# Hybrid state-space, attention and expert layer in fp32: the order of loads and small operations in the opening, and the rotation angles ahead of the q and k norms

## The reference, cut to what matters

```python
xn = rms_norm(h, norm1_g)                    # rows of x scaled by 1/sqrt(mean square), times g
z = xn @ w_in                                # 1024 x 4096
u, q, k, v, g_ssm, g_att = split(z)          # 512 each for u, q, k, v, 1024 each for the gates
dt = exp(log_dt)                             # 32 groups of 64 states
abar = exp(a_re * dt) * (cos(a_im * dt) + i sin(a_im * dt))
bbar = (abar - 1) / a * b                    # complex
state[l] = abar * state[l-1] + bbar u[l]     # per group, along the tokens
y_ssm = Re(c state) + d * u, gelu, gated
q, k = rms_norm(q), rms_norm(k)              # per head and half, 64 wide
y_att = (softmax(q1 k1) - lam * softmax(q2 k2)) v
h = h + (sig(g_ssm) * (y_ssm @ w_proj_ssm) + sig(g_att) * (y_att @ w_proj_att)) @ w_out
y = h + experts(rms_norm(h))                 # 32 experts, 4 per token, swiglu
```

## Time and profile before

| what | value |
|---|---|
| median of three runs | 1146.06 us (1145.76 to 1146.14) |
| span of the profiled execution, first to last instruction | 1142.5 us |
| that execution's own time | not listed apart from the three runs; the median is 3.6 us above its span |
| PE busy | 1095.7 us (96%) |
| DVE, ACT, POOL busy | 298.4, 166.3, 34.1 us |
| DMA | 435.13 MB, mean 381 GB/s |
| chain that ended last | PE 58%, DMA 38%, DVE 2%, ACT 1% |

### The profile page before, as it was taken

How to read it: one execution, slowest core, us unless ns; L and a number is a source line. 1 busy time by engine, 2 the same in 40 slices (tenths; PEclk the granted TensorE clock), 3 DMA queues, 4 the chain that set the end, 5 groups by cost and what they waited for, 6 DMA issues and landing times.

```text
span 1142.5 us, 14277 instructions
## 1 busy us (share of the span) xinstructions
PE 1095.7 (96%) x5292; PEld 446.9 (39%) x5292; DVE 298.4 (26%) x804; ACT 166.3 (15%) x343; POOL 34.1 (3%) x51
## 2 busy tenths in 40 slices
PE   7999999999999999999999999999999999999997
PEld 4468887633333333333333333333333333333332
DVE  5987244242111111111111111111111111111111
ACT  3043440221111111111111111111111111111110
POOL 6020010000000000000000000000000000000000
PEclk9999999999999999999999999999999999999999
DMA  8734489999999999999999999999999999999996
GB/s 229 200 123 87 140 284 352 366 361 403 427 428 427 429 430 427 429 430 428 428 430 429 427 430 427 428 430 427 428 430 428 427 430 429 427 430 429 427 428 269
DMA packets 63578, 435.13 MB, mean 381 GB/s; under 512 B 19856, under 2 KB 28096, under 8 KB 38592
## 3 DMA queue, kind: packets, MB, share of 16 engines
q1 hardware_dynamic: 57776, 433.17, 92.6%
q0 software_dynamic: 608, 1.34, 0.6%
q10 hardware_dynamic: 5168, 0.27, 0.3%
HBM read 432.01 MB, written 1.57 MB: 380 GB/s over the span
## 4 chain that ended last, share of the span: by engine, by line
PE 58%; DMA 38%; DVE 2%; ACT 1%; issue 1%; SPq 0%; DVEq 0%; ACTq 0%
DMA arena<-in_w_up 38%; PE bank L1066 23%; PE bank L1111 9%; PE bank L635 5%; PE bank L673 4%; PE bank L619 3%; PE bank L1010 2%; PE bank L995 2%; PE bank L949 2%; PE bank L873 1%; PE bank L858 1%; PE bank L846 1%; DMA arena<-in_w_in 1%; PE bank L805 1%; PE bank L937 1%
## 5 line engine op out<-in xcount | busy, mean ns | idle before, releaser
L1066 PE MATMUL bank<-arena 128*64 128x512 f32 x2048 | 452.6, 594 | 30.2 <-DMA arena<-in_w_up 29.9
L1066 PEld LDWEIGHTS bank<-arena 128*64 128x64 f32 x2048 | 143.7, 137 | 331.8 <-issue 271.5
L1111 PE MATMUL bank<-arena 128*64 128x512 f32 x1024 | 226.8, 595 | 0.0
L1809 DVE TENSOR_SCALAR arena<-bank 128x256 f32<-128x256 f32 x64 | 27.2, 425 | 499.1 <-PE bank L1066 499.1
L1111 PEld LDWEIGHTS bank<-arena 128*64 128x64 f32 x1024 | 70.7, 137 | 133.9 <-issue 133.1
L1367 ACT ACTIVATE arena<-arena 128x256 f32<-128x256 f32 x64 | 26.6, 417 | 451.7 <-DVE arena L1810 451.7
L619 PEld LDWEIGHTS bank<-arena 128*128 128x128 f32 (+1 forms) x450 | 49.2, 143 | 89.6 <-issue 82.1
L619 PE MATMUL bank<-arena 128*128 128x128 f32 (+1 forms) x450 | 75.2, 290 | 8.9 <-DMA arena<-in_x 5.1
L1010 PE MATMUL bank<-arena 64*128 64x512 f32 x256 | 63.9, 616 | 0.7 <-ACT arena L1375 0.7
L995 PE MATMUL bank<-arena 128*64 128x512 f32 x248 | 60.1, 605 | 0.0
L1774 DVE TENSOR_SCALAR arena<-arena 128x128 f32 (+3 forms) x126 | 33.3, 327 | 92.7 <-issue 92.6
(11 more groups left out here) (294 smaller groups left out, 517.0 us busy)
## 6 DMA issues: line engine op xcount, KB each, us to landing
arena<-in_w_up SPq DMA_DIRECT2D x125, 2048.0 KB, 25.5
arena<-in_w_down SPq DMA_DIRECT2D x63, 2048.0 KB, 26.8
arena<-in_w_in SPq DMA_DIRECT2D x16, 1024.0 KB, 6.0
arena<-in_w_up SPq DMA_DIRECT2D x5, 1024.0 KB, 6.4
arena<-in_w_out SPq DMA_DIRECT2D x4, 1024.0 KB, 7.8
arena<-in_w_proj_ssm SPq DMA_DIRECT2D x8, 256.0 KB, 5.8
arena<-in_w_proj_att SPq DMA_DIRECT2D x2, 1024.0 KB, 7.9
arena<-in_w_down SPq DMA_DIRECT2D x2, 1024.0 KB, 31.6
```

What stands on the lines that cost most here:

```text
L1066: last = pe.matmul(B[n][64 * h:64 * h + 64, :], xg[:, 2 * j + r, :], rows[r][2 * h + n], start=False, stop=(j == order[-1] and r == 1), sk ...
L1111: last = pe.matmul(B[3][64 * n:64 * n + 64, :], (actT_last if last_block else actT)[:, k % 4, k // 4, :], dn_w[parity][k // 4][:, k % 4, 5 ...
L1809: TS(part(glu_t, n), v[:, 0], LIMIT, None, ALU.min)
```

## The change

ACT's queue: g is loaded as 8 rows of 128 (`g1_rows`, 512 bytes each); a_re, a_im and log_dt follow on the same queue and leave SP's. The first activation is Exp, and the Exp of dt stands ahead of the squares. The b loads are issued together after both roots. x_scale is copied after the wait for `trig` and the two Exps.

SP: token tile 0, first half of piece 0 (row blocks 0, 1; semaphore first_in), second half (2, 3), token tile 1, piece 1, then the c tables.

PE: turns g first, turns tile 0, runs piece 0 on tile 0 (block by block as the halves arrive), turns the small tables, then tile 1, and then runs piece 0 on it.

DVE: copies g out of the bank; a*dt stands between the products of tile 0 and tile 1; the lambda sums stand ahead of CR and CI; e8 and the angles n = 1 to 8 stand between WI and the norms of q and k, and n = 15 stays behind them.

```diff
@@ sync @@
-            for t in range(TT):
+            def load_x(t):
                 sp.dma_start(hx[:, t, :], a["x"][0, P * t:P * t + P, :]).then_inc(x_in[t], 16)
+            load_x(0)
+            for dst, src in first_pairs():
+                sp.dma_start(dst, src).then_inc(s["first_in"], 16)
             for dst, src in piece(0):
                 sp.dma_start(dst, src).then_inc(slot_in[0], 16)
-            for src, o in ((a["ssm_a_re"], 0), (a["ssm_a_im"], 1)):
-                sp.dma_start(natA[0:GG, o, :], src[0].rearrange("(g t) p -> g (t p)", t=2))\
-                  .then_inc(s["a_in"], 16)
-            sp.dma_start(dts[0:GG], a["ssm_log_dt"][0].rearrange("(g t) -> g t", t=2))\
-              .then_inc(s["a_in"], 16)
+            load_x(1)
+            for dst, src in piece(1):
+                sp.dma_start(dst, src).then_inc(slot_in[1], 16)
@@ tensor @@
+            pe.wait_ge(s["g1_in"], 16)
+            pe.transpose(B[7][:, 0:KT], g1_rows[0:KT, :], ident[0:KT, 0:KT]).then_inc(s["g1_ps"], 1)
...
-            z_piece(0, xT, 0, 0)
+            pe.wait_ge(s["xT"], 1)
+            pe.wait_ge(s["first_in"], 16)
+            for k in range(4):
+                if k == 2:
+                    piece_arrived(0)
+                pe.matmul(B[0][:, :], xT[:, k, 0:P], halves(0)[:, k, :], start=(k == 0), stop=False)
             pe.wait_ge(s["aT_in"], 1)
             transposes([(B[4][:, GG * i:GG * i + GG], natA[0:GG, i, :]) for i in range(4)])\
                 .then_inc(s["aT_ps"], 1)
-            pe.wait_ge(s["xT"], 4)
+            turn_x(1)
+            pe.wait_ge(s["xT"], 3)
             z_piece(0, xT, 1, 1)
@@ scalar @@
-            act.dma_start(g1, a["norm1_g"][0].rearrange("(k p) -> p k", p=P),
-                          allow_slow_non_contiguous=True).then_inc(s["g1_in"], 16)
+            act.dma_start(g1_rows[0:KT, :], a["norm1_g"][0].rearrange("(k p) -> k p", p=P)).then_inc(s["g1_in"], 16)
+            for src, o in ((a["ssm_a_re"], 0), (a["ssm_a_im"], 1)):
+                act.dma_start(natA[0:GG, o, :], src[0].rearrange("(g t) p -> g (t p)", t=2))\
+                    .then_inc(s["a_in"], 16)
+            act.dma_start(dts[0:GG], a["ssm_log_dt"][0].rearrange("(g t) -> g t", t=2))\
+                .then_inc(s["a_in"], 16)
             act.wait_ge(s["warm"], 1)
-            act.activation(warm, warm, ACT.Sqrt)
+            act.activation(warm, warm, ACT.Exp)
+            act.wait_ge(s["a_in"], 48)
+            act.activation(dts[0:GG], dts[0:GG], ACT.Exp).then_inc(s["dt"], 1)
...
             act.wait_ge(s["trig"], 1)
             act.activation(mg[:, 0, :], pa[:, 2, :], ACT.Exp)
             act.activation(mg[:, 1, :], pa[:, 2, :], ACT.Exp, scale=float(L))
+            act.wait_ge(s["scale_ps"], 1)
+            act.activation(x_scale, B[7][:, 0:TOK], ACT.Copy).then_inc(s["x_rs"], 1)
@@ vector @@
+            dve.wait_ge(s["g1_ps"], 1)
+            link(dve.tensor_copy(g1, B[7][:, 0:KT]))
+            for half in range(2):
+                turned(0, half)
             dve.wait_ge(s["dt"], 1)
...
             last.then_inc(s["aT_in"], 1)
+            x_variance(0)
+            for half in range(2):
+                turned(1, half)
+            x_variance(1)
...
             TTo(WIv, tAw, tBw, ALU.add).then_inc(s["win_t"], 1)
 
+            dve.wait_ge(s["xn"], 4)
+            link(dve.tensor_copy(e8r, cs))
+            link(dve.tensor_copy(e8i, sn))
+            for _ in range(3):
+                cmul(t16[0], t16[1], e8r, e8i, e8r, e8i, (GG,), scratch_2)
+                dve.tensor_copy(e8r, t16[0])
+                link(dve.tensor_copy(e8i, t16[1]))
...
+            for n in (1, 2, 4, 8):
+                angles(n)
 
             dve.wait_ge(s["q_sq"], 4)
...
+            angles(15)
```

More of the change, by code:

```diff
@@ L61 @@
  sig act aT2_ps aT2 ysb summed up_used dn_used bup_used dsel fin fin_out wr_in loop_z u_turn
- ahead_in up_tail dn_tail wg gated first_rows row_left row_right cT g1_in gate_ps out_ps rank routed o_read row_used up_half warm""".split()
+ ahead_in up_tail dn_tail wg gated first_rows row_left row_right cT g1_in gate_ps out_ps rank routed o_read row_used up_half warm g1_ps first_in""".split()
 def mixer_and_experts(nc, a, out):
@@ L208, in mixer_and_experts @@
         natA = at(158, 4, P)
+        g1_rows = at(199, P)
         lamrow = at(198, 4, SUB)
@@ L278, in piece @@
             slot = slot_of(i)
+            if i == 0:
+                w = a["w_in"][0].rearrange("(k p) n -> p k n", p=P)
+                return [(halves(0)[:, 2:4], w[:, 2:4, 0:512])]
             if i < 8:
@@ L301, in piece, with first_pairs @@
             return [(halves(i), w[:, 4 * (c % 2):4 * (c % 2) + 4, 512 * (c // 2):512 * (c // 2) + 512])]
+        def first_pairs():
+            w = a["w_in"][0].rearrange("(k p) n -> p k n", p=P)
+            return [(halves(0)[:, 0:2], w[:, 0:2, 0:512])]
         def pv(i):
@@ L359, in _ @@
                 arrived = last_in if i == PIECES - 1 else slot_in[i % RING]
-                if i > 0:
+                if i > 1:
                     for dst, src in piece(i):
                         sp.dma_start(dst, src).then_inc(arrived, 16)
-                else:
+                elif i == 0:
                     for n, half in enumerate((a["ssm_c_re"], a["ssm_c_im"])):
@@ L622, in _, with turn_x @@
             pe.wait_ge(s["ident"], 1)
-            for t in range(TT):
+            pe.wait_ge(s["g1_in"], 16)
+            pe.transpose(B[7][:, 0:KT], g1_rows[0:KT, :], ident[0:KT, 0:KT]).then_inc(s["g1_ps"], 1)
+            def turn_x(t):
                 pe.wait_ge(x_in[t], 16)
@@ L628, in _ @@
                         .then_inc(s["xT_ps"], 1)
-            pe.wait_ge(s["xT"], 2)
+            turn_x(0)
             def z_piece(i, tokens, bank, t):
@@ L653, in _ @@
                             for i in range(4)]).then_inc(s["cT_ps"], 1)
+            pe.wait_ge(s["xT"], 4)
             for t in range(TT):
@@ L1151, in _ @@
                 act.activation(xr[:, t:t + 1], xs[:, t:t + 1], ACT.Sqrt).then_inc(s["x_rs"], 1)
[L1152 to L1159, removed]
+            for dst, src in ((br_raw, a["ssm_b_re"]), (bi_raw, a["ssm_b_im"])):
+                act.dma_start(dst, src[0].rearrange("(g t) p h -> (t p) g h", t=2)).then_inc(s["b_in"], 16)
             act.wait_ge(s["trig"], 1)
@@ L1407, in turned, with x_variance @@
                     .then_inc(s["xT"], 1)
[L1409 to L1412, removed]
+            def x_variance(t):
                 x_rms = xs[:, t:t + 1]
@@ L1428, in _ @@
             last.then_inc(s["aT_in"], 1)
+            x_variance(0)
+            for half in range(2):
+                turned(1, half)
+            x_variance(1)
+            dve.wait_ge(s["x_rs"], 2)
+            for t in range(TT):
+                last = TS(diag[:, t, :], ident, xr[:, t:t + 1], None, ALU.mult)
+            last.then_inc(s["diag"], 1)
             dve.wait_ge(s["aT_ps"], 1)
@@ L1501, in _ @@
             cmul(bbr, bbi, br_raw, bi_raw, per_pair(cfr, H), per_pair(cfi, H), (GG, H))
+            dve.wait_ge(s["lam_in"], 64)
+            for i in range(2):
+                last = dve.tensor_tensor_reduce(lamrow[:, 2 * i, :], lamrow[:, 2 * i, :],
+                                                lamrow[:, 2 * i + 1, :], 1.0, 0.0, ALU.mult, ALU.add,
+                                                lamv[:, 2 + i:3 + i])
+            last.then_inc(s["lam_e"], 1)
             dve.wait_ge(s["cp_zero"], 1)
@@ L1532, in _, with angles @@
             TTo(WIv, tAw, tBw, ALU.add).then_inc(s["win_t"], 1)
[L1534 to L1539, removed]
+            dve.wait_ge(s["xn"], 4)
[5 more added lines that the diff above has]
+                link(dve.tensor_copy(e8i, t16[1]))
+            dve.memset(Rr[:, :, 0], 1.0)
+            dve.memset(Ri[:, :, 0], 0.0)
+            dve.tensor_copy(Rr[:, :, 1], e8r)
+            link(dve.tensor_copy(Ri[:, :, 1], e8i))
+            def angles(n):
+                cmul(Rr[:, :, n + 1:2 * n + 1], Ri[:, :, n + 1:2 * n + 1], Rr[:, :, 1:n + 1], Ri[:, :, 1:n + 1],
+                     per_pair(Rr[:, :, n], n), per_pair(Ri[:, :, n], n), (GG, n), scratch_2)
+            for n in (1, 2, 4, 8):
+                angles(n)
             dve.wait_ge(s["q_sq"], 4)
```

1 line of the change is left out of this document (removed).

## The result

The changed kernel takes 1158.39 us, the median of 4 runs (1157.75 to 1160.32), against 1145.91 (1145.29 to 1146.14) for the kernel before in the same comparison: ratio 1.0106, 95% interval 1.0093 to 1.0119. It is 12.5 us slower; the forecast was 1158.4. The profiled execution took 1157.75 us with a span of 1156.0.

The account below looks back on a forecast made before the run. DVE's norms, by 0.7 us over PE, were taken to bind at PE's turning of WR and WI. PE starting 10.4 later plus 1.9 for the clock gave +12.3: 1142.5 + 12.3 + 3.6 = 1158.4 us, range 1151.0 to 1160.5.

Parts of the forecast that it names:

- PE's lead at the end of gate tile 1: Opening: PE starts piece 0 sooner and gains 0.5 to 1.5 us, taken as 1.0, kept until it leaves gate tile 1.
- DVE's first product: Opening: DVE's first product, at 20.41 us in the kernel before, comes at about 19.2.
- block with POOL holding DVE: After win_t at 64.8: e8, squarings and angles, 8.1 us before, held by POOL's memset and copies, end at 79.2.
- norms behind it: After the angles: DVE's q and k norm work takes 5.7 us and ends at 84.9.
- PE starts turning: Turning of WR and WI: PE starts at 85.0 instead of 74.56, 10.4 us later.
- clock, over 40 blocks: Turning after about 12 us idle: PE resumes at 1.2 GHz and loses 1.9 us, bounds 1.0 and 2.6.
- shift of the span: Whole kernel: later PE start of 10.4 plus clock loss of 1.9 makes +12.3 us.
- The rival that the angles are hidden: PE's wait at 73.85: norms done before PE leaves gate tile 1, opening's gain kept, 1144.4 us; chance of faster 0.06.
- The rival without it: Moved block: DVE not held by POOL, PE starts at 78.7, +4.1 and +1.9 for the clock, 1152.1 us; chance 0.15.
- The rival that turning keeps the clock low: Turning: transposes do not raise the clock, all 40 blocks run slow, 4.4 us instead of 1.9, 1160.9 us; chance 0.03.
- DVE's long chain gains 1.2: Opening: DVE's long chain of products starts 1.2 us earlier, bounds 0 and 2.0.
- Uniform shift: From PE's start at 74.56 on: everything, expert loads included, moves by the same amount; w_up waits keep their length.

Follow-up runs that it names:

- experiment 1: Changed kernel with e8 and angles n = 1 to 8 moved back behind the q and k norms: 1144.01 us, ratio 0.9984 to the kernel before.
- experiment 2: Kernel before, with only the block of e8 and angles n = 1 to 8 put ahead of the norms: 1159.26 us, ratio 1.0117.
- experiment 3: Changed kernel with POOL's memset of MM and four copies also waiting for the root of the norms' variance: 1152.01 us, ratio 1.0052.
- experiment 9: Changed kernel with 32 unread products of 128x256 on PE while it waits for win_t: 1157.13 us, ratio 1.0092 to the kernel before.
- experiment 7: Changed kernel with the angles back behind the norms and the second b load issued behind both Sin: 1142.90 us, ratio 0.9973.
- experiment 10: Changed kernel, angles still ahead of the norms, with the second b load behind both Sin and five unread PE products ahead of x: 1156.53 us, ratio 1.0083.
- experiment 5: Kernel before, with only the wait for lambda and its two sums moved ahead of CR and CI: 1145.17 us, ratio 0.9992.
- experiment 6: Changed kernel with the angles behind the norms and the lambda sums back behind the release of win_t: 1145.66 us, ratio 0.9994.
- experiment 4: Changed kernel with 26 unread products of 128x256 on PE while it waits for win_t: 1158.34 us, ratio 1.0103 to the kernel before.
- experiment 8: Changed kernel with angles behind the norms, second b load behind both Sin, and five unread PE products ahead of token tile 0: 1141.88 us, ratio 0.9968.

## Why the prediction was right, step by step

| step | forecast | measured |
|---|---|---|
| PE's lead at the end of gate tile 1 | 1.0 | 1.31 |
| DVE's first product | 19.2 | 20.22 |
| block with POOL holding DVE | 14.4 | 14.7 (65.79 to 80.47) |
| norms behind it | 5.7 | 5.73 |
| PE starts turning | 85.0 | 86.34 |
| clock, over 40 blocks | 1.9 | 1.67 |
| shift of the span | 12.3 | 13.5 |
| time | 1158.4 | 1158.39 |

**What decides.** PE waits at this point for DVE's products with the norms, and an engine's block moved ahead of the work that another waits for costs its whole length. Experiments 1 and 2 show that from both sides. The rival that the angles are hidden falls with them.

**The hold by POOL.** The rival without it (1152.1) fell; experiment 3 gives its case by taking POOL away, and it takes 1152.01. That figure, too, hits closer than its parts: PE turns there at 80.35, and the rival had 78.7. The pattern was as forecast down to the operation: the first copy passes, the second waits for the memset's end, and two operations pass per POOL copy. The Trainium skill (SBUF — State Buffer, Who interferes with whom) has this rule for copies, and the trace agrees: 3.49 beside the memset, 0.18 without it (experiment 3).

**The clock.** The size was right, and experiment 9 shows the cause. The rival that turning keeps the clock low fell, and with it what the Trainium skill (TensorE: Matmul & The Clock Gate, Part 4: PE-mode transpose) says: in the changed kernel the clock rose while PE did nothing but turn blocks. Windows of the changed kernel:

```profile
74.00:76.00 2.00, 0.00 (x0) 0.00 (x0) 1.77 (x16) 0.00 (x0) 0.00 (x0) 1.00 0.92 234
76.00:78.00 2.00, 0.00 (x0) 0.00 (x0) 1.81 (x17) 0.00 (x0) 0.00 (x0) 0.53 0.74 259
...
88.00:90.00 2.00, 2.00 (x12) 2.00 (x11) 1.90 (x10) 1.27 (x4) 0.00 (x0) 0.55 0.00 0
90.00:92.00 2.00, 2.00 (x21) 2.00 (x20) 0.94 (x4) 2.00 (x5) 0.00 (x0) 1.00 0.06 16
```

PE stopped at 72.54, and from 76 on the clock is at its lower level, 1.2 GHz; it is back at 2.4 GHz in the window from 90.

**What failed: DVE's opening.** The term "DVE's long chain gains 1.2" was mis-sized; it measured 0.2. The angle reduction ended even earlier than I had it (16.12 for 16.8). But I had the two b loads issued together ahead of the Exps and gave that no price. The issue of the second held ACT for 2.67 us, so the table for the Exps was loaded only behind it, and the lead was gone. It was inside my bounds (0 to 2.0). Experiment 7 shows the cause, and experiment 10 that such a lead reaches PE's turning 1:1 (1.83 and 1.87). The remaining 0.3 lies in the block.

**Two errors that cancelled.** The sum in spans is 1.2 too small (12.3 for 13.5). Against that I added 3.6 us to come from the profiled span to the median, and in the changed kernel the median is only 2.4 above it (1158.39 and 1156.0). With that gap my sum gives 1142.5 + 12.3 + 2.4 = 1157.2; that the figure hit to the hundredth is luck. Every execution on record takes 1.7 to 1.9 more than its own span, and one of the kernel before with the same span of 1142.5 took 1144.28. So the profiled execution of before was some 1.8 quicker than its median, the changed kernel's only 0.6 (1157.75), and the loss is 12.5 between medians but 13.5 between profiles. One place where the kernel before was quick can be seen: tile 0's eight records took 3.67, and 5.17 and 5.66 in experiments 2 and 5 with the same opening. That this makes up the 1.8 is argued, not shown.

**Uniform shift.** In the changed kernel the steps from 74.56 on moved together, expert loads included: 11.78 + 1.67 = 13.45, and w_up is 13.45 later. Nothing on this chain had slack to catch it. That need not hold for small shifts: the first long wait for w_up is 24.63 in the kernel before and 24.64 in the changed one, but 25.33 in experiment 1 and 25.14 in experiment 10, where up to 0.7 us gained ahead of it was lost again.

## What to carry to other kernels

Before moving small operations of one engine ahead of others, see who waits for those others, and add up at their prices in the new place: here 8.1 us of operations of 0.17 became 14.7 beside a POOL memset and four copies, and an idle PE paid with its clock as well. Where two engines are level at a meeting point, freeing one may give nothing that can be measured (experiments 5 and 6); look at both (experiment 1). Before adding to a profile's span, see by how much an execution's own time exceeds its own span.

## What the runs showed of the hardware that was not expected

The time that PE stays slow in the opening differs from execution to execution of nearly the same code. Tile 0's eight records took 3.67 (before), 4.38 (changed), and 5.53, 5.17, 5.48, 4.34, 5.66, 5.45, 5.12 and 4.67 (experiments 1 to 7 and 9). With five small products ahead of them they took 3.70 and 3.78 (experiments 8 and 10). Eight transposes of x still took 1.97 in experiment 8. The prediction says that the granted clock has no record that early. It has one, and it reads 1.00 in the windows of all these openings, so it doesn't show the slow stretch. The runs of the kernel before spread over 1143.98 to 1148.81 on that chip, those of experiment 8 over 1141.50 to 1142.96. That the spread comes from this alone is argued, not shown.

The clock did not fall after the same idle time twice. In experiment 4 PE stopped at 83.73, and at 86 the clock was low, 2.3 us later. In the changed kernel PE stopped at 72.54, and the window up to 76, 3.5 us later, still reads 1.00.

The issue of the second b load (64-byte elements), right behind the first, held ACT's queue for 2.67 us in the changed kernel and for 1.99, 2.57, 3.44, 2.06 and 3.42 in experiments 1, 3, 4, 6 and 9. It began between 13.5 and 14.8 and ended between 16.5 and 17.2 in all six. Behind both Sin it took 0.41, 0.48 and 0.74, begun at 17.30, 16.08 and 16.16 (experiments 7, 8 and 10). What it waits for until then no run shows.
